# Two mixer blocks on one core: reordering the steps of the differential attention on ScalarE and VectorE

## What is computed

```python
def diff_attention_group(q, k, v, z, ...):
    q = rmsnorm(q.reshape(b, t, 4, 2, 64), q_gain) * 64 ** -0.5     # k alike, without the factor
    ...
    s = einsum('bqhcd,bkhcd->bhcqk', q_blk, k)                      # c: two score matrices per head
    p = softmax(where(mask, s, neg))
    wts = p[:, :, 0] - lam * p[:, :, 1]
    o = einsum('bhqk,bkhv->bqhv', wts, v)                           # q_blk: 128 queries at a time
    ...
    return rmsnorm(o, out_gain) * (1 - lambda_init) * silu(z)

def gated_delta_rule(q, k, v, g, beta):
    lmat = I + strict_lower(k_beta @ k.T * decay)                   # per chunk
    u, w = solve_triangular(lmat, [v_beta, k_beta * exp(gc)])
    v_new = u - w @ state; o = (q * exp(g)) @ state + a_qk @ v_new  # chunk after chunk
    state = state * exp(g_last) + k_dec.T @ v_new
```

## Time and profile before

| | before |
|---|---|
| median of 3 runs | 2049.99 us (2049.94 to 2050.85) |
| the profiled execution | 2050.15 us, of which the span of the trace is 2048.4 us |
| TensorE busy | 1994.2 us, 97% of the span |
| VectorE, ScalarE, GpSimd busy | 863.3, 735.9, 936.8 us |
| granted TensorE clock, mean | 0.995 of full speed |
| rounds 2 and 3 with the differential steps | from about 212 to 372 us of the span |

### The profile page before, as it was taken

The page is one execution under the profiler, slowest core; times in us unless marked ns, Lnnn a source line. Parts: engine busy times, 40 slices in busy tenths (PEclk is TensorE's granted clock), DMA queues, the critical chain, the costliest instruction groups (busy, mean ns, idle before and its releaser), DMA issues.

```text
span 2048.4 us, 30374 instructions
## 1 busy us (share of the span) xinstructions
PE 1994.2 (97%) x11366; PEld 1704.6 (83%) x11366; DVE 863.3 (42%) x1502; ACT 735.9 (36%) x1116; POOL 936.8 (46%) x1220
## 2 busy tenths in 40 slices
PE   7999988999999999999999999999999999999998
PEld 6688666799999999688888888888888888888887
DVE  7744665742222222996443233343343452222112
ACT  5543444432222223634444233333333332222222
POOL 5432211454444564554332545444444564545564
PEclk9999999999999999999999999999999999999999
DMA  5211100122222223222111322222222223222232
GB/s 186 83 62 42 42 32 32 50 95 85 93 88 92 97 99 114 73 83 79 58 61 52 109 72 88 83 78 83 84 77 77 91 90 102 92 92 93 103 103 83
DMA packets 49754, 168.68 MB, mean 82 GB/s; under 512 B 6400, under 2 KB 8576, under 8 KB 49664
## 3 DMA queue, kind: packets, MB, share of 16 engines
q1 hardware_dynamic: 46192, 161.37, 23.4%
q10 hardware_dynamic: 3472, 6.03, 0.9%
HBM read 165.29 MB, written 2.10 MB: 82 GB/s over the span
## 4 chain that ended last, share of the span: by engine, by line
PE 87%; DVE 8%; ACT 2%; issue 1%; DMA 1%; ACTq 0%; DVEq 0%
PE slot L2013 86%; DVE ix_score L1835 1%; DVE square L1770 1%; DVE score L1500 0%; DVE x_lo L1788 0%; DVE xt L1780 0%; ACT score L1041 0%; PE slot L2150 0%; DMA h<-x_t 0%; PE slot L2185 0%; PE slot L2448 0%; DVE dqk L1343 0%; DMA w_raw<-weights 0%; DVE aq L1773 0%; DVE ak L1773 0%
## 5 line engine op out<-in xcount | busy, mean ns | idle before, releaser
L2529 POOL TENSOR_TENSOR w_lo<-w_raw,w_hi 128x256 fp32r<-128x256 f32 x1216 | 936.6, 802 | 1100.9 <-ACT w_hi L814 848.4
L2013 PE MATMUL slot<-x_hi,w_hi 128*128 128x264 f32 (+1 forms) x1864 | 643.9, 345 | 3.5 <-ACT dqk L1007 3.4
L2013 PE MATMUL slot<-x_hi,w_lo 128*128 128x264 f32 (+1 forms) x1864 | 630.5, 338 | 0.0
L2013 PE MATMUL slot<-x_lo,w_hi 128*128 128x264 f32 (+1 forms) x1864 | 628.8, 337 | 0.0
L2013 PEld LDWEIGHTS slot<-x_hi,w_hi 128*128 128x128 f32 x1864 | 351.4, 189 | 50.7 <-issue 7.9
L2013 PEld LDWEIGHTS slot<-x_lo,w_hi 128*128 128x128 f32 x1864 | 350.9, 188 | 39.2
L2013 PEld LDWEIGHTS slot<-x_hi,w_lo 128*128 128x128 f32 x1864 | 351.7, 189 | 37.8 <-issue 1.4
L814 ACT ACTIVATE w_hi<-w_raw 128x1024 fp32r<-128x1024 f32 x216 | 226.4, 1054 | 321.4 <-PE slot L2013 311.6
L2013 PE MATMUL slot<-f_hi,w_hi 128*128 128x264 f32 (+2 forms) x550 | 173.5, 316 | 0.0
L2013 PE MATMUL slot<-f_hi,w_lo 128*128 128x264 f32 (+2 forms) x550 | 173.3, 315 | 0.0
L2013 PE MATMUL slot<-f_lo,w_hi 128*128 128x264 f32 (+2 forms) x550 | 172.9, 314 | 0.0
(11 more groups left out here) (342 smaller groups left out, 2819.3 us busy)
## 6 DMA issues: line engine op xcount, KB each, us to landing
w_raw<-weights SPq DMA_DIRECT2D x304, 512.0 KB, 3.2
h<-x_t ACTq DMA_DIRECT2D x4, 512.0 KB, 6.1
dec<-decays ACTq DMA_DIRECT2D x4, 264.0 KB, 3.2
const<-consts SPq DMA_DIRECT2D x1, 576.0 KB, 6.4
at_rot<-rotations ACTq DMA_DIRECT2D x1, 528.0 KB, 5.1
ix_rot<-rotations ACTq DMA_DIRECT2D x1, 528.0 KB, 6.6
rt_rot<-rotations ACTq DMA_DIRECT2D x1, 528.0 KB, 3.7
out<-h SPq DMA_DIRECT2D x2, 256.0 KB, 2.2
```

The lines of the kernel that those rows point to most:

```text
L2013: return nc.tensor.matmul(out, lhsT, rhs, start=start, stop=stop)
L2529: nc.gpsimd.tensor_tensor(w_lo[j][:, piece], w_raw[j][:, piece], w_hi[j][:, piece].bitcast(F32), ALU.subtract).then_inc(s_lo, 1)
```

## The change

Nothing is computed otherwise; instructions trade places.

- On ScalarE `chains` is cut up. At a point the order is now: probability copy, rsqrts, drains, `w_split`, squares and Silus, exponentials.
- On VectorE the maxima of step s stand ahead of the scaling of step s-1.
- Squares of q and k heads are made at `norm_point` - 1 instead of `norm_point`, and those of head outputs at `HO_POINT` - 1, so two points ahead of their sum. For the attention's heads 4 to 6 `HO_POINT` itself goes one up (from 50, 58, 66 to 51, 59, 67): their squares stay at the same point, the sum, the rsqrt and the product move one point back.

```diff
--- before.py
+++ after.py
@@ -267,7 +267,7 @@
 assert dense_done(("dv", 1)) + 1 < DF_START
 
 
-HO_POINT = {**{n: POINTS * (n + 1) + 2 for n in range(NQ - 1)}, **{4 + j: DF_START + 8 * j + 14 for j in range(3)}}
+HO_POINT = {**{n: POINTS * (n + 1) + 2 for n in range(NQ - 1)}, **{4 + j: DF_START + 8 * j + 15 for j in range(3)}}
 LATE_HEADS = [3, 7]
 SILU_POINT = {23 + 2 * j: j for j in range(4)}
 HEADS_OUT = [4, 5, 6, 0, 1, 2, 3, 7]
@@ -990,7 +990,8 @@
 
                 p = point[0]
                 point[0] += 1
-                chains(p)
+                prob_copy(p)
+                rsqrts(p)
                 for key in ASIDE_DENSE:
                     if dense_done(key) == p:
                         name, j = key
@@ -1006,23 +1007,29 @@
                             src, dst = src.rearrange("p (a t) -> p a t", a=2), sz[:, :, j, :]
                         A.sig(nc.scalar.activation(dst, src, ACT.Copy), *evac_at(key))
                 w_split(BLOCK[ASIDE_DENSE[0]] + aside_blocks(p + 1) + RING - 1)
-
-            def chains(p):
-
-                for i in norm_at(p, 0):
-                    A.sync()
-                    squares([dqk[:, i, :]])
+                all_squares(p)
+                exps(p)
+
+            def rsqrts(p):
+
                 for i in norm_at(p, 2):
                     rsqrt(("hn", 8 + i), 1.0 / 64, T)
                 for i, first in HO_POINT.items():
-                    if p == first and i < 4:
+                    if p == first + 2:
+                        rsqrt(("ho", i), 1.0 / P, T)
+
+            def all_squares(p):
+
+                for i in norm_at(p, -1):
+                    A.sync()
+                    squares([dqk[:, i, :]])
+                for i, first in HO_POINT.items():
+                    if p == first - 1 and i < 4:
                         A.sync()
                         squares_chunk(i)
-                    elif p == first:
+                    elif p == first - 1:
                         wait_evac(act, ("PV", i - 4, NQ - 1))
                         squares([dqk[:, i - 4, :]])
-                    elif p == first + 2:
-                        rsqrt(("ho", i), 1.0 / P, T)
                 if p in SILU_POINT:
                     made["table"] = None
                     j = SILU_POINT[p]
@@ -1030,6 +1037,9 @@
                     if j == 3:
                         A.sync()
                         act.sem_inc(s_silu, 1)
+
+            def exps(p):
+
                 if p < DF_START or (p - DF_START) % 2 == 0:
                     return
                 s = df_at(p, 0)
@@ -1040,6 +1050,11 @@
                     for c in range(2):
                         A.sig(nc.scalar.activation(Sx[i][c][:, 0:w], Sx[i][c][:, 0:w], ACT.Exp, bias=mx[i][:, c:c + 1],
                                                    accum_out=sums_[i][:, c:c + 1]), s_dfa, 2 * s + c + 1)
+
+            def prob_copy(p):
+
+                if p < DF_START or (p - DF_START) % 2 == 0:
+                    return
                 e = df_at(p, 2)
                 if e is not None:
                     w = (e % NQ + 1) * P
@@ -1474,20 +1489,6 @@
                         head_scaled(i, dqk[:, i - 4, :])
                 if p < DF_START or (p - DF_START) % 2 == 0:
                     return
-                e = df_at(p, 1)
-                if e is not None:
-
-                    j, n, i = e // NQ, e % NQ, e % 2
-                    w = (n + 1) * P
-                    dve.wait_ge(s_dfa, 2 * e + 2)
-                    V.own(nc.vector.reciprocal(sums_[i][:], sums_[i][:]))
-                    V.sync()
-                    V.own(nc.vector.tensor_scalar(sums_[i][:, 1:2], sums_[i][:, 1:2], lamt[:, 5:6], None, ALU.mult))
-                    V.sync()
-                    V.own(nc.vector.tensor_scalar(Sx[i][1][:, 0:w], Sx[i][1][:, 0:w], sums_[i][:, 1:2], None, ALU.mult))
-                    V.sync()
-                    V.sig(nc.vector.scalar_tensor_tensor(Pm[i][:, 0:w], Sx[i][0][:, 0:w], sums_[i][:, 0:1], Sx[i][1][:, 0:w],
-                                                         ALU.mult, ALU.add), s_dfp, e + 1)
                 s = df_at(p, 0)
                 if s is not None:
                     j, n, i = s // NQ, s % NQ, s % 2
@@ -1502,6 +1503,20 @@
                         V.own(ins) if c == 0 else V.sig(ins, *evac_at(key))
                     V.sync()
                     V.sig(nc.vector.tensor_scalar(mx[i][:], mx[i][:], -1.0, None, ALU.mult), s_df, 2 + s)
+                e = df_at(p, 1)
+                if e is not None:
+
+                    j, n, i = e // NQ, e % NQ, e % 2
+                    w = (n + 1) * P
+                    dve.wait_ge(s_dfa, 2 * e + 2)
+                    V.own(nc.vector.reciprocal(sums_[i][:], sums_[i][:]))
+                    V.sync()
+                    V.own(nc.vector.tensor_scalar(sums_[i][:, 1:2], sums_[i][:, 1:2], lamt[:, 5:6], None, ALU.mult))
+                    V.sync()
+                    V.own(nc.vector.tensor_scalar(Sx[i][1][:, 0:w], Sx[i][1][:, 0:w], sums_[i][:, 1:2], None, ALU.mult))
+                    V.sync()
+                    V.sig(nc.vector.scalar_tensor_tensor(Pm[i][:, 0:w], Sx[i][0][:, 0:w], sums_[i][:, 0:1], Sx[i][1][:, 0:w],
+                                                         ALU.mult, ALU.add), s_dfp, e + 1)
                 e = df_at(p, 3)
                 if e is not None:
                     j, n = e // NQ, e % NQ
```

## The result

The changed kernel takes 2032.87 us (median of 4 runs, 2032.32 to 2034.10) against 2049.97 us of the kernel before in the same session: a ratio of 0.9919, 95% interval 0.9907 to 0.9931, or 17.1 us less. The forecast was 2033.4 us. The profiled execution took 2034.1 us with a span of 2032.3 us, 16.1 us under that of before; it is the longest of the four, and the others, at a mean granted clock of 0.998 instead of 0.997, are 1.0 to 1.8 us shorter.

The account below looks back on a forecast made before the run. TensorE, busy 97%, loses time waiting on ScalarE's queue blocked by exponentials, and at lower clock behind gaps. 7.8 + 5.0 + 2.5 + 3.4 - 0.6 - 1.5 = 16.6 us off the 2048.4 us span: 2033.4 us, range 2030 to 2042.5.

Parts of the forecast that it names:

- one of the five small: Five shorter TensorE stalls for the probability copy in rounds 2 and 3, 3.1 us together; 2.8 us expected back.
- Probability copy: ScalarE's odd points: copying ahead of the exponentials ends TensorE's transpose waits in rounds 2 and 3, gaining 7.8 us.
- three large stalls: TensorE's copy waits of 1.62, 1.62 and 2.05 us (last at points 67 and 68): gains 1.65, 1.6, 1.75 us.
- what is late next: After the earlier copy, transposes need VectorE's scaling, ending about 247.15 instead of 245.73; `Z` then starts just behind the subtraction.
- Drain: Point 51: draining ahead of the exponentials removes 3.3 of a 3.42 us gap and a 1.7 us slow stretch: 5.0 us.
- Heads' products a point later: Head 4's product leaves point 53: round 3's decays 0.8 us earlier, gap 2.25 to 1.5, slow stretch gone: 2.5 us.
- gap at point 68: The sum of squares moved from 67 to 68, 1.02 us, was to fill what remained of the 2.05 us stall.
- Squares ahead: Points 35 to 39: no gain, 0.6 us lost before round 2, gaps merge to 1.95 us, slow stretch costs 1.5.
- The clock: Slow stretches behind gaps of 3.42, 2.25, 2.05 us go (1.7, 1.7, 3.4 us); a new one at point 39 costs 1.5.
- Rival 1: Stalls go but the clock does not follow, more than one gap causing slow stretches: 11.3 us gained, 2038.7 us, chance 0.2.

Follow-up runs that it names:

- e1: The kernel before with only the probability copy moved to the head of ScalarE's odd points: 2039.78 us, ratio 0.9949.
- e3: The changed kernel with VectorE's scaling of step s-1 ahead of the maxima of step s again: 2034.19 us.
- e5: The changed kernel with sum, rsqrt and product of heads 4 to 6 back at their old points, squares unmoved: 2031.32 us.
- e2: The kernel before with only drains and weight casts moved ahead of the exponentials, probability copy still behind them: 2044.76 us, ratio 0.9973.
- e7: e6 with the exponential that frees the spread decays' bank taken ahead of that of `DT`: 2029.52 us.
- e12: e7 with the points of heads 4 to 6 put back as in e5: 2029.06 us, ratio 0.9900 to the kernel before.
- e4: The changed kernel with the squares of q and k heads back at `norm_point`: 2031.60 us.
- e8: The kernel before, unchanged, profiled again: one run, 2049.34 us.
- e9: The changed kernel, unchanged, profiled again: 2033.91 us.
- e6: e4 with the table of exponentials and logarithms loaded right behind round 1's last Silu (point 29): 2029.48 us.

## Why the prediction was right, step by step

The time lies 0.5 us from the forecast, the profiled span (2032.3 us) 0.5 us on the other side of the forecast span (2031.8). 11.3 us of the forecast were idle time and 5.3 the clock; measured are 10.6 and 5.1. The terms, read from TensorE's starts of `Z`, of the output matmuls and of the last PV in both profiles:

| stretch of TensorE's program | before | changed | gain | forecast |
|---|---|---|---|---|
| round 2: decays to the second `Z` (points 36 to 40) | 20.79 | 22.55 | -1.76 | -0.6 - 1.5 |
| second to third `Z` (42) | 7.99 | 7.41 | 0.58 | one of the five small |
| third to fourth (44) | 8.88 | 7.37 | 1.51 | 1.65 |
| fourth to fifth (46) | 7.64 | 7.35 | 0.29 | one of the five small |
| fifth to outputs (48 to 52) | 28.46 | 22.78 | 5.68 | 5.0 and a small one |
| outputs to round 3's first `Z` (53 to 56) | 21.86 | 19.82 | 2.04 | 2.5 |
| round 3: second to third `Z` (60) | 9.58 | 8.02 | 1.56 | 1.6 |
| third to fourth (62) | 8.30 | 7.74 | 0.56 | one of the five small |
| fourth to fifth (64) | 7.68 | 7.39 | 0.29 | one of the five small |
| fifth to last PV (66 to 72) | 29.54 | 24.55 | 4.99 | 1.75 + 3.4 |

- **Probability copy.** The three large stalls gave 1.51, 1.56 and, less 3.4 for the clock, 1.6 us, where 1.65, 1.6 and 1.75 were put. The small ones give 0.58, 0.29, 0.56 and 0.29, and one more inside the fifth line, 2.4 together; 2.8 was a little high. At point 46 the subtraction (its end is 256.53, `Z` starts at 256.62) holds `Z` back, at point 62 the new wait of 0.6 us for an rsqrt's bank takes what the copy gave. e1 confirms the mechanism with this move alone, at 6.1 us of rest against 7.8 + 0.3 in the theory. It lacks 0.25 us at point 44, where the scores wait for the maxima, and 1.1 at point 60, where `Z` waits for an rsqrt. e3 shows that VectorE's swap is worth 1.7 us in the changed kernel, 0.9 of it at points 39 and 40, 0.3 at 44 and 0.5 before round 3's first `Z`; the wait at 60 is in neither e3 nor e5, and no run shows which move takes it away. The forecast gave the swap only the role of what is late next and no price of its own.
- **Drain.** 5.68 us less 1.7 for the clock are 4.0, of which 3.3 were put on the drain and some 0.7 on the small stall at 50. Right; e2 has 2.6 and 3.7 for it in all, and in this line alone 28.46 less 23.42 us, which is 3.3 without the clock.
- **Heads' products a point later.** The gap for `dn_qg` fell by 0.66 us (forecast 0.8), but of the 2.04 us of that line up to 1.7 are the clock, so 0.3 to 0.5 arrived (0.48 by e5). And e5, which puts this part alone back, has the smaller rest. The failed step is that the sum of squares was taken to fill a gap at point 68 that would be there otherwise; e5 shows no gap there. The forecast also did not see the wait of 0.6 us for the rsqrt's bank. This term should have stood at -0.5 us (changed against e5) or -1.1 (e7 against e12) instead of +0.8.
- **Squares ahead.** The wait at 39 is 1.97 us (forecast 1.95), with the slow stretch behind it (1.7 us; 1.5 put in). The loss at the start of round 2 was put at 0.6; it is 0.3 up to the first `Z` (10.46 us before, 10.75 changed). Up to point 40 it seems to be 0.1, as of the 1.76 us of the first line the clock is 1.7, though e4 finds 0.7 us by taking these squares back. What hides the loss is VectorE's swap: without it (e3) the stretch from the first to the second `Z` takes 11.08 us, with it and the clock up as well (e5) 10.16. The chunk's square also left point 38; no run shows its part.
- **The clock.** Three stretches gained and one lost, as put, and e8 and e9 show the same again for both kernels. The size was right for these two kernels. The rule behind it, that the length of the gap decides between 1.62 and 2.05 us, is wrong by e1, e2, e3, e5 and their repeats; the three gaps that cost 6.8 us closed or shrank, but that the one of 1.59 us left the clock up and the one of 1.97 brought it down, as put, was luck. The forecast also passed over a fourth slow stretch of before, behind the last PV, of 1.7 us behind gaps of at most 1.47 us, which stays in the changed kernel and so did no harm to the sum. Rival 1, that more than the one gap is behind a slow stretch, had the better reason.

The Trainium skill (TensorE: Matmul & The Clock Gate, HAM oscillation) has idle gaps between bursts drop the clock. The traces agree in the direction, since each slow stretch from 200 us to the last PV follows a gap of 1.6 us or more and the one behind it a row of shorter gaps; they do not show it as a rule for the single gap, as one of 3.15 us left the clock at 2.4 GHz.

## What to carry to other kernels

Where an engine runs its queue in order, look for what stands behind a wait and was ready long before: the wait of the bound engine is then put down to a short copy, and the cause is the instruction ahead of it. Move such copies and drains to the front, and price what becomes late next from the same time line, for every engine whose order changes; but work that only prepares (squares for a later norm) goes behind whatever the chain still needs, and it pays to count what a moved step puts into an already full stretch. Time at a lower clock behind gaps is worth taking into a forecast as a range, with a repeated profile to show how far it is fixed.

## What was not expected of the hardware

The same program, with the same gap of TensorE to 0.01 us, has the clock at 2.4 GHz behind a gap of 3.15 us in one execution and at a mean of 0.72 over the 6 us behind it in another. In these kernels of 2030 to 2050 us such stretches took 0 to 6.8 us of a profile before the last PV and 0 or 1.7 behind it, and the runs of the kernel before scatter from 2047.0 to 2053.3 us. What fixes it when the gap does not stays open. Of two table loads of 1.28 us each on ScalarE, taken out together (e6 against e4), the one that ScalarE could make while VectorE prepared its next input gave nothing, and the one ahead of an rsqrt with copies behind it gave 1.4 us of rest.
